# A two-block transformer forward pass: an earlier copy in the MLP's fast product, additions one granule ahead, and GpSimd making part of the weights' low parts

## The reference

```
def sq_relu_mlp(x, w_up, w_down):        # x 256 x 1024, w_up 1024 x 4096, w_down 4096 x 1024
    h = jax.nn.relu(x @ w_up)
    return (h * h) @ w_down

h = h + rms_norm(sq_relu_mlp(rms_norm(h, mpre), w_up, w_down), mpost)
```

## Time and profile before

| | |
|---|---|
| runs shown | 1120.95, 1121.07, 1121.63 us |
| profiled execution: its own time | 1121.05 us |
| its span, first to last instruction | 1119.2 us |
| mean granted TensorE clock | 0.993 of full speed |
| TensorE matmuls busy | 1098.5 us (98%) |
| VectorE busy | 833.0 us (74%) |
| ScalarE busy | 653.6 us (58%) |
| GpSimd busy | 157.1 us (14%) |

### The profile page before, as it was taken

The page is one execution under the profiler, slowest core; times in us unless marked ns, Lnnn a source line. Parts: engine busy times, 40 slices in busy tenths (PEclk is TensorE's granted clock), DMA queues, the critical chain, the costliest instruction groups (busy, mean ns, idle before and its releaser), DMA issues.

```text
span 1119.2 us, 12927 instructions
## 1 busy us (share of the span) xinstructions
PE 1098.5 (98%) x5107; PEld 911.4 (81%) x5107; DVE 833.0 (74%) x944; ACT 653.6 (58%) x805; POOL 157.1 (14%) x119
## 2 busy tenths in 40 slices
PE   9999999999999999999999999989999999998997
PEld 7788888888888888888888888868788888886886
DVE  5785768775677884778458569997668976899972
ACT  7656476645877743645687465644556546656551
POOL 1435600000434310000032000000015000000000
PEclk9999999999999999999999999989999999998999
DMA  9644434554555554655335465458845424746670
GB/s 355 247 178 165 168 134 165 210 189 170 194 205 194 196 191 177 266 183 208 138 131 204 148 244 188 155 163 235 310 171 206 146 100 169 252 162 188 150 264 37
DMA packets 31368, 211.46 MB, mean 189 GB/s; under 512 B 3720, under 2 KB 3888, under 8 KB 6864
## 3 DMA queue, kind: packets, MB, share of 16 engines
q1 hardware_dynamic: 28464, 196.66, 48.2%
q0 software_dynamic: 2848, 14.03, 5.6%
HBM read 209.62 MB, written 1.05 MB: 188 GB/s over the span
## 4 chain that ended last, share of the span: by engine, by line
PE 77%; DVE 15%; ACT 3%; DMA 3%; issue 1%; SPq 0%; DVEq 0%; ACTq 0%
PE ps L759 65%; DVE Wl L1993 6%; DVE htmp L2554 6%; DMA raw<-in_wstream 3%; PE ps L1212 3%; PE aux L830 2%; ACT Wh L1433 2%; PE ps L1214 1%; DVE hTl L2563 1%; PE ps L873 1%; PE aux L1079 1%; PE aux L1249 1%; PE aux L1064 1%; PE ps L950 0%; PE aux L1236 0%
## 5 line engine op out<-in xcount | busy, mean ns | idle before, releaser
L759 PE MATMUL ps<-Wh,xT 128*128 128x512 f32 x1792 | 560.1, 391 | 0.0
L1993 DVE TENSOR_TENSOR Wl<-raw,Wh 128x2048 fp32r<-128x2048 f32 x189 | 435.5, 2315 | 139.9 <-ACT Wh L1433 138.9
L1433 ACT ACTIVATE Wh<-raw 128x2048 fp32r<-128x2048 f32 x189 | 359.6, 1914 | 168.6 <-PE ps L759 151.1
L759 PEld LDWEIGHTS ps<-Wh,xT 128*128 128x128 f32 x1792 | 336.4, 188 | 69.7 <-issue 0.3
L759 PE MATMUL ps<-Wl,xT 128*128 128x512 f32 x896 | 348.6, 389 | 0.0
L759 PEld LDWEIGHTS ps<-Wl,xT 128*128 128x128 f32 x896 | 168.3, 188 | 34.1
L2554 DVE STREAM_TRANSPOSE htmp<-held 32x512 f32<-32x512 f32 x128 | 90.0, 703 | 2.7
L759 PE MATMUL ps<-Wh,hTh 128*128 128x512 f32 x192 | 77.3, 402 | 12.4 <-ACT ps L1878 10.8
L759 PE MATMUL ps<-Wl,hTh 128*128 128x512 f32 x192 | 76.5, 399 | 0.0
L759 PE MATMUL ps<-Wh,hTl 128*128 128x512 f32 x192 | 76.3, 397 | 0.0
L759 PEld LDWEIGHTS ps<-Wh,hTh 128*128 128x128 f32 x192 | 37.2, 194 | 21.8 <-ACT ps L1878 11.6
(11 more groups left out here) (387 smaller groups left out, 1434.3 us busy)
## 6 DMA issues: line engine op xcount, KB each, us to landing
raw<-in_wstream SPq DMA_DIRECT2D x183, 1024.0 KB, 4.7
raw<-in_wstream POOLq DMA_DIRECT2D x8, 1024.0 KB, 8.0
grow<-in_post_gains POOLq DMA_DIRECT2D x4, 512.0 KB, 5.7
grow<-in_b_gate POOLq DMA_DIRECT2D x6, 256.0 KB, 3.5
mrows<-in_mem SPq DMA_DIRECT2D x2, 512.0 KB, 5.3
raw<-in_wstream SPq DMA_DIRECT2D x2, 512.0 KB, 6.6
x<-in_x SPq DMA_DIRECT2D x1, 1024.0 KB, 13.7
out<-x SPq DMA_DIRECT2D x4, 256.0 KB, 2.0
```

Of the source, the lines that this page charges most:

```text
L759: mm = nc.tensor.matmul(ps[2 * pair + t][:, :], a[:, kt, t * P:(t + 1) * P], w[:, slot, j, :], start=(first and j == 0 and q == 0), stop=( ...
L1433: nc.scalar.activation(split_view(Wh, g), weight_view(raw, g), ACT.Copy).then_inc(hi_ready, 1)
L1993: nc.vector.tensor_tensor(split_view(Wl, g), weight_view(raw, g), split_view(Wh, g).bitcast(F32), ALU.subtract).then_inc(lo_ready, 1)
```

## The change

1. **The copy of the first product.** In ScalarE's order, `fast_copy("Q1", ...)` is moved from the loop over the fast product to the last upward unit, ahead of the high part of the third pair (pair 2) and of unit 7's square.
2. **Additions one granule ahead.** ScalarE's copy after Q7 and VectorE's `add_parts` move from k = 10 to k = 9, each ahead of its step for granule 29 (high part on ScalarE, low part on VectorE).
3. **Low parts on GpSimd.** `plan_pooled` names 14 granules per MLP whose low part GpSimd makes: 5, 7, 9, 11, 13, 15 of the upward product and 17, 19, 21, 23, 25, 28, 30, 32 of the downward one. VectorE skips them. They are counted on a semaphore of their own (`lo_pool`), and whoever waits for a low part (`wait_low`: TensorE, SP, GpSimd) waits for the count of the engine that makes it. On GpSimd the low parts and the accumulating transfers stand in one loop in the order of the granules, so that a transfer's wait holds back the low parts behind it.

```diff
+def plan_pooled():
+    pooled = []
+    for m in range(2):
+        pooled += range(P0[f"up{m}_0"] + RING + 1, P0[f"down{m}_0"], 2)
+        pooled += [P0[f"down{m}_0"] + k for k in (1, 3, 5, 7, 9, 12, 14, 16)]
+    return pooled
+def low_count(p):
+    by_pool = p in POOLED
+    return by_pool, sum((k in POOLED) == by_pool for k in range(p + 1))
...
+        def wait_low(eng, g):
+            by_pool, n = low_count(g)
+            eng.wait_ge(lo_pool if by_pool else lo_ready, n)
...
             for g in range(RING, NP):
                 if not ADDED[g]:
-                    sp.wait_ge(lo_ready, g + 1 - RING)
+                    wait_low(sp, g - RING)
...
-            def added_weights(name):
-                for g in range(P0[name], P1[name]):
-                    if ADDED[g]:
-                        pool.wait_ge(lo_ready, g + 1 - RING)
-                        pool.dma_start(raw[:, g % RING, :, :], wstream[SRC[g]], accum_op=ALU.add)\
-                            .then_inc(added[CHAIN[g]], 16)
+            def split(g):
+                pool.wait_ge(hi_ready, g + 1)
+                nc.gpsimd.tensor_tensor(Wl[:, g % RING, :, :], raw[:, g % RING, :, :], Wh[:, g % RING, :, :].bitcast(F32),
+                                        ALU.subtract).then_inc(lo_pool, 1)
+            def weights(first, end):
+                for g in range(first, end):
+                    if g in POOLED:
+                        split(g)
+                    if g + RING < NP and ADDED[g + RING]:
+                        wait_low(pool, g)
+                        pool.dma_start(raw[:, g % RING, :, :], wstream[SRC[g + RING]], accum_op=ALU.add)\
+                            .then_inc(added[CHAIN[g + RING]], 16)
...
-            added_weights("down0_0")
+            weights(P0["up0_0"], P1["down0_1"])
...
                 for n in range(8):
                     up(n)
+                    if n == 7:
+                        wait_drained(act, f"up{m}_7", 1)
+                        fast_copy("Q1", bank(n1, 0), bank(n0, 0), -1.0)
                     if n >= 3 and n % 2:
                         high_pair((n - 3) // 2)
                     squared_rows(n)
...
                 for k in range(len(FAST_ORDER) - 1):
-                    if k == AT["Q1"]:
-                        fast_copy("Q1", bank(n1, 0), bank(n0, 0), -1.0)
-                    elif k == AT["Q6"]:
+                    if k == AT["Q6"]:
                         fast_copy("Q6", bank(n1, 1), bank(n1, 0), -1.0)
-                    elif k == AT["Q7"]:
+                    elif k == AT["Q7"] - 1:
                         fast_copy("Q7", partz[:, :], bank(n1, 1), 1.0)
...
             def split(g, i=None):
-                if g >= NP:
+                if g >= NP or g in POOLED:
                     return
...
-                    elif k == AT["Q7"]:
+                    elif k == AT["Q7"] - 1:
                         add_parts()
                     split(P0[n0] + k + RING)
```

More of the change, by code:

```diff
@@ L139 @@
 CHAIN = {P0[n] + AT[what]: int(what == "Q7") for n in FAST for what in ("Q5", "Q6", "Q7", "Q4")}
+def plan_pooled():
[4 more added lines that the diff above has]
+    return pooled
+POOLED = plan_pooled()
+def low_count(p):
+    by_pool = p in POOLED
+    return by_pool, sum((k in POOLED) == by_pool for k in range(p + 1))
 def landed_count(p):
@@ L501, in build @@
         lo_ready = sem("lo_ready")
+        lo_pool = sem("lo_pool")
         gran_used = sem("gran_used")
@@ L745, in _ @@
             after_mix("p4", "x5", (3, reads("mobao1", 1)))
-            added_weights("down1_0")
+            weights(P0["up1_0"], P1["down1_1"])
             after_mix("p5", None, None)
@@ L764, in granule @@
             def granule(slot, lo_value, th, tl, kts, pair, first, last, read_out, seeded=False):
-                pe.wait_ge(lo_ready, lo_value)
+                if lo_value is not None:
+                    pe.wait_ge(lo_ready, lo_value)
                 for t in range(2):
@@ L790, in product @@
                         before[g - P0[name]]()
-                    granule(g % RING, g + 1, th, tl, kts_of(name, g), U[name] % 2, g == P0[name], g == P1[name] - 1,
+                    wait_low(pe, g)
+                    granule(g % RING, None, th, tl, kts_of(name, g), U[name] % 2, g == P0[name], g == P1[name] - 1,
                             bank_free or bank_read(name))
@@ L802, in tile_by_tile @@
                         if t == 0:
-                            pe.wait_ge(lo_ready, g + 1)
+                            wait_low(pe, g)
                         if g == P0[name]:
@@ L1348, in mlp @@
                 for g in range(P0[f"down{m}_1"], P1[f"down{m}_1"] - RING):
-                    granule(g % RING, g + 1, hTh, hTl, TILES[g], U[f"down{m}_1"] % 2, False, False, None, True)
+                    wait_low(pe, g)
+                    granule(g % RING, None, hTh, hTl, TILES[g], U[f"down{m}_1"] % 2, False, False, None, True)
                 tile_by_tile(steps_of([f"down{m}_1"], (hTh, hTl)),
@@ L1866, in high_pair @@
                             .then_inc(sem("h_hi"), 1)
[L1868 to L1872, removed]
                 n0, n1 = f"down{m}_0", f"down{m}_1"
@@ L1878, in fast_copy @@
                     nc.scalar.activation(dst, src, ACT.Copy, scale=scale).then_inc(sem("fast_copy"), 1)
+                for n in range(8):
+                    up(n)
+                    if n == 7:
+                        wait_drained(act, f"up{m}_7", 1)
+                        fast_copy("Q1", bank(n1, 0), bank(n0, 0), -1.0)
+                    if n >= 3 and n % 2:
+                        high_pair((n - 3) // 2)
+                    squared_rows(n)
                 def fast_part(what, b, dst):
```

## The result

The changed kernel takes 1130.09 us in the median (1129.95 to 1131.32, 6 runs) against 1121.13 before, 0.8% more: 1.0082 of the time before, 95% interval 1.0072 to 1.0093. The span grew from 1119.2 to 1128.1 us. Lines have moved: L791 and L1351 are TensorE's products (before L759 and L1317), L1468 ScalarE's weight copy, L2029 VectorE's low parts, L737 GpSimd's, L747 its accumulating transfers, L2590 the transposes, L2599 a pair's low part, L2660 the mixed rows' low part, L1900 a pair's high part, L1908 the copies of the fast product.

A forecast was written before the change was run, and what follows sets the result against it. It took VectorE's queue as the bound, TensorE running into it at granule 17 once per MLP (10.8 us in two waits). Step delays of +4.9 and 0.7, said +5 per MLP, gave 1121 + 10 = 1131 us, range 1124 to 1139.

The forecast's parts named there:

- The copy, worth nothing by itself: Earlier ScalarE copy removes 7.7 us at granule 17, but 3 return at once, the rest at granules 21, 23 and 29.
- The additions: Additions moved ahead of granule 29's low part remove 1.1 us there in the first MLP, 0.46 in the second.
- The price on GpSimd: One low part of 2048 elements on GpSimd takes 4.5 us, with bounds 3.8 and 5.0.
- The exclusion: VectorE's two-input subtractions and GpSimd's shut one another out; each GpSimd low part blocks VectorE up to 4.5 us, transposes pass.
- The steps: First MLP reckoned instruction by instruction, each engine waiting for the other: granule 29 starts at 795.8, about +5 us per MLP.
- The 1.3 at granule 18: TensorE wants low part 18 at 740.8, VectorE ends it at 742.1: 1.3 us lost.
- The 0.5 at granule 28: The accumulating transfer for granule 28 lands 10.5 us after issue, so its GpSimd low part costs TensorE 0.5 us.
- the 0.7 for low part 32: Low part 32, last in GpSimd's queue, adds 0.7 us per MLP.
- The slow clock at granule 20: A 5.7 us stall before granule 20 brings 2.3 us of slow TensorE clock again.
- its +4.9: Delay of granule 29 in the first MLP: 795.8 against 790.9 by the same reckoning over the kernel before.
- The faster one: Rival, chance 0.28: GpSimd's subtractions cost VectorE nothing, granule 29 starts 7.2 us earlier per MLP, 1107 us.
- The flat one: Rival, chance 0.12: GpSimd gives way halfway, mutual waits cost VectorE what it is relieved of, 1121 to 1123 us.

The follow-up runs named there:

- e1: Kernel before with only the earlier copy and the earlier additions, VectorE making all low parts: 1121.06 us, 0.9999 of the kernel before.
- e6: e5 with the copy of the first product put back behind pair 2's high part, additions still one granule ahead: 1104.94 us, 0.9857 of the kernel before.
- e3: Changed kernel, but GpSimd fills its 28 low parts with zeros twice each, reading nothing from SBUF: 1105.36 us, 0.9864 of the kernel before.
- e7: Changed kernel, but GpSimd copies raw to Wl twice instead of subtracting, one SBUF input per instruction: 1117.67 us, 0.9970 of the kernel before.
- e4: Changed kernel, but each GpSimd low part is two instructions of 1024 elements: 1121.27 us, 1.0008 of the kernel before.
- e5: Changed kernel with 4 low parts per MLP on GpSimd (granules 13, 16, 20, 21) in place of 14: 1103.00 us, 0.9841 of the kernel before.

## Why the prediction was right

- **What bounds the kernel.** VectorE's queue. e1 shows that the stall could not be bought off on ScalarE, and e6 that it nearly vanishes by itself when VectorE is in time.
- **The copy, worth nothing by itself.** Said: 3 us back at granule 20, the rest at 21, 23 and 29. Measured in e1: 3.24 there, 0.93, 1.27 and 1.19 at these three, and no change of the time.
- **The additions.** Said: the 1.1 at granule 29 goes. By itself the edit did not do that: in e1 a wait for low part 29, 1.19, stands in its place. In the kernel after there is none at 29, but TensorE comes there 4.15 later, so that no run shows this term as the edit's own.
- **The price on GpSimd.** 4.5 from the earlier trace rows, measured 4.62.
- **The exclusion.** Read off for up to 1024 elements; it holds for 2048 (the kernel after), goes away with the reads (e3 against e7), and costs less with half the length (e4), though there VectorE is not let in at every place.
- **The steps.** Pair 1 turned at 721.1: its high part starts at 720.87. Pair 2 at 744.9: 745.02. Mixed rows' low part done at 758.7: 758.79. Granule 23 loses 1.7: 1.92. Granule 17 loses 2.1: 2.38. Granule 29 at 795.8: 795.62.
- **Sizes that were off.** The 1.3 at granule 18 is not there in the first MLP: the low clock behind the wait at 17 (1.6) stands in its place; in the second MLP it is 1.06, and the clock stays up there. The 0.5 at granule 28 did not come: the accumulating transfer lands 7.9 to 8.3 after its issue in the kernel after, not 10.5, and low part 28 is there in time. Nor did the 0.7 for low part 32: TensorE has no wait behind granule 29. The slow clock at granule 20 costs 1.9 rather than 2.3. And the reckoning put granule 29 of the kernel before 0.6 too early, so that its +4.9 was 4.15 in the trace; the second MLP lost 4.86. In all 9.0 for the 10 forecast. That it came so near is in part luck: steps that did not come (1.3, 0.5 and 0.7 in the first MLP) and one that was not foreseen (the low clock behind granule 17, 1.6) partly offset each other.
- **The rivals.** The faster one was given 1107 if GpSimd cost VectorE nothing; e3, where that is so (with 3.7 for a low part in place of 4.6), takes 1105. The flat one was given 1121 to 1123 for an instruction that lets VectorE in halfway; e4, which does so in the upward product, takes 1121. Both prices were near, and neither applied, since GpSimd reads, and holds VectorE off to the end of an instruction. The faster rival also named the place that decides, whether low part 13 starts before or behind low part 12; in e5 it starts behind, and low part 12 loses nothing.

## What to carry to other kernels

Work that is taken off a bounding engine is worth the time by which that engine gets ahead, not the work that it no longer does: ask which of its remaining instructions share something with the one that has moved, and where in its fixed order these stand. Offload to GpSimd what can lie beside VectorE's transposes, behind a two-input instruction and not in front of one; four low parts in such places brought 18 us, the same number elsewhere cost 11. And before an early release is built, look whether the engine behind it is on time for the next thing: an earlier copy, here, only changed the name of the wait.

## What was not expected

TensorE's clock does not answer to a short wait in the same way each time. In the kernel after, idle time of 2.38 before granule 17 in the first MLP is followed by matmuls at 0.43 us apart (granted clock 0.79 in the 8 us from 733), while 2.36 at the same place in the second MLP is followed by matmuls at 0.23 (1.00 in the 7 us from 1027); after 5.23 and 5.45 the clock was low both times. What tells the two apart was not tried.
